# S5 + FoX decoder step: second memory weights among u's reads, output matrices between memory panels, last Toeplitz rows on two queues

## The reference, cut to what matters

```
mem_pairs = [mem_kv(mem_prompt, mem_norm[l], w_mem_kv[l]) for l in range(2)]   # rmsnorm(mem) @ w, 256 memory tokens
z = rmsnorm(x) @ w_in[0]; u = z[:, :768] as 48 groups of 16 channels
ar, ai, bbr, bbi = s5_discretize(...)            # 48 groups x 64 complex states
bu = einsum('btgc,gpc->btgp', u, bb)             # input to the state
h  = associative_scan over t of  h = a*h + bu    # complex
y  = einsum('btgp,gcp->btgc', hr, c_re) - einsum(..., hi, c_im) + d_skip*u
y  = gelu(y); y = y * sigmoid(y @ w_glu + b_glu)
```

## Time and profile before

| | us |
|---|---|
| Median of 3 runs (lowest, highest) | 1526.56 (1525.75, 1530.57) |
| The profiled execution | 1528.19 |
| Its span in the trace | 1526.4 |
| TensorE matmuls busy | 1418.7 (93%) |
| VectorE busy | 976.9 (64%) |
| ScalarE busy | 577.0 (38%) |
| GpSimd busy | 638.6 (42%) |
| Mean granted TensorE clock | 0.965 |

### The profile page before, as it was taken

The page is one execution under the profiler, slowest core; times in us unless marked ns, Lnnn a source line. Parts: engine busy times, 40 slices in busy tenths (PEclk is TensorE's granted clock), DMA queues, the critical chain, the costliest instruction groups (busy, mean ns, idle before and its releaser), DMA issues.

```text
span 1526.4 us, 32537 instructions
## 1 busy us (share of the span) xinstructions
PE 1418.7 (93%) x12097; PEld 1316.3 (86%) x12097; DVE 976.9 (64%) x1658; ACT 577.0 (38%) x1019; POOL 638.6 (42%) x420
## 2 busy tenths in 40 slices
PE   6986868989999999999899989998989999999997
PEld 6984758979999999999789966557889999999997
DVE  5759967576773177766658688662677761377755
ACT  4544354344342143423434235431444331234313
POOL 1686332304344334432269878302223443344430
PEclk9997789999999999999899999999999999999999
DMA  5344463213333232332236679994213233223321
GB/s 173 117 113 79 66 174 114 87 41 97 95 100 97 74 96 85 104 96 71 73 99 188 201 197 310 317 323 137 69 56 95 83 103 90 82 86 93 103 82 62
DMA packets 289082, 180.47 MB, mean 118 GB/s; under 512 B 54248, under 2 KB 274572, under 8 KB 288924
## 3 DMA queue, kind: packets, MB, share of 16 engines
q1 hardware_dynamic: 288412, 179.07, 40.8%
q10 hardware_dynamic: 576, 0.13, 0.0%
HBM read 167.10 MB, written 10.63 MB: 116 GB/s over the span
## 4 chain that ended last, share of the span: by engine, by line
PE 70%; DVE 14%; issue 9%; ACT 2%; DMA 2%; SPq 1%; POOL 1%; DVEq 0%; ACTq 0%; POOLq 0%
PE big L2641 57%; PE big L2707 3%; PE misc L2792 2%; PE big L2738 1%; DVE tmp L1253 1%; DVE y L1730 1%; DVE rstd L1211 1%; DVE x L1736 1%; DVE w_lo L1200 1%; DVE x_lo L1243 1%; PE misc L2762 1%; SPq L591 1%; ACT yc L2498 1%; PE big L2990 1%; PE misc L3207 1%
## 5 line engine op out<-in xcount | busy, mean ns | idle before, releaser
L941 POOL TENSOR_TENSOR w_lo<-raw,w_hi 128x1024 fp32r<-128x1024 f32 (+2 forms) x153 | 393.8, 2574 | 714.2 <-ACT w_hi L2136 553.8
L2136 ACT ACTIVATE w_hi<-raw 128x1024 fp32r<-128x1024 f32 (+2 forms) x179 | 198.5, 1109 | 586.7 <-PE big L2641 538.8
L2641 PE MATMUL big<-x_hi,w_hi 128*128 128x264 f32 x1984 | 406.7, 287 | 8.3 <-DVE uc L1819 2.8
L2641 PE MATMUL big<-x_hi,w_lo 128*128 128x264 f32 x1984 | 400.8, 283 | 0.0
L2641 PE MATMUL big<-x_lo,w_hi 128*128 128x264 f32 x1984 | 398.8, 283 | 0.0
L2641 PEld LDWEIGHTS big<-x_hi,w_hi 128*128 128x128 f32 x1984 | 305.9, 189 | 13.0 <-issue 4.8
L2641 PEld LDWEIGHTS big<-x_lo,w_hi 128*128 128x128 f32 x1984 | 305.6, 189 | 0.0
L2641 PEld LDWEIGHTS big<-x_hi,w_lo 128*128 128x128 f32 x1984 | 305.3, 189 | 0.0
L1823 DVE SCALAR_TENSOR_TENSOR yc<-uc,convw,yc 128x512 f32<-128x512 f32 x88 | 136.7, 1553 | 113.2 <-ACT yc L2498 113.2
L2641 PE MATMUL big<-h_hi,w_hi 128*128 128x264 f32 x616 | 125.0, 284 | 6.3 <-DVE h_lo L1838 6.3
L2641 PE MATMUL big<-h_lo,w_hi 128*128 128x264 f32 x616 | 123.9, 282 | 0.0
(11 more groups left out here) (432 smaller groups left out, 2335.3 us busy)
## 6 DMA issues: line engine op xcount, KB each, us to landing
raw<-in_w_up SPq DMA_DIRECT2D x88, 512.0 KB, 3.9
raw<-in_w_down SPq DMA_DIRECT2D x32, 704.0 KB, 4.7
areas<-in_cache_v SPq DMA_DIRECT2D x42, 384.0 KB, 4.9
areas<-in_cache_k SPq DMA_DIRECT2D x41, 384.0 KB, 4.4
raw<-in_w_in SPq DMA_DIRECT2D x16, 512.0 KB, 4.3
raw<-in_w_out SPq DMA_DIRECT2D x16, 512.0 KB, 4.2
raw<-in_w_kv SPq DMA_DIRECT2D x12, 512.0 KB, 4.3
spare<-in_cache_k SPq DMA_DIRECT2D x12, 384.0 KB, 4.4
```

The costliest lines, as they stand in the source:

```text
L941: pool.tensor_tensor(w_lo[slot][:, 0:kb, :], raw[slot][:, 0:kb, :], w_hi[slot][:, 0:kb, :].bitcast(F32), ALU.subtract).then_inc(lo_made, 1)
L2136: A.activation(w_hi[slot][:, 0:kb, :], raw[slot][:, 0:kb, :], ACT.Copy).then_inc(hi_made, 1)
L2641: ins = pe.matmul(big[2 * slot + b_][:, 0:c1 - c0], w[slot][:, k, :], r[:, c0:c1], start=(k == 0 and n_ == 0), stop=(k == kb - 1 and n_ == 2))
```

## The change

Three things move; none is added or taken away.

1. On SP, the load of memory panel 13 stands between the fifth and the sixth of u_load(0)'s ten reads instead of behind them.
2. On VectorE, the six operations of the first third's `cp` go into the loop over the memory panels: the first behind the read of panel 12, the second behind that of 13, two behind 14 and two behind 15 (`CP_AT`). In the first four turns the `mem_lo` of the fourth comes ahead of the read-and-round step of that turn's next panel. The two row_max of scores 0 and 1, which followed `cp`, now follow the first six products of the scan of third 0.
3. In the last third, SP issues the first four toep rows (16 to 64 KB) and ScalarE the last four (80 to 128 KB), right after its copies of `kern`.

```
+U_AHEAD = 5
+CP_AT = {4: (0,), 5: (1,), 6: (2, 3), 7: (4, 5)}
+ACT_TOEP = 4
-            def u_load(t):
+            def u_load(t, between=None):
                 g = slice(t * TG, t * TG + TG)
                 for tau in range(CHUNK):
+                    if tau == U_AHEAD and between is not None:
+                        between()
...
-            u_load(0)
-            weights("memkv1", mem_w[1], start=1)
+            u_load(0, lambda: weights("memkv1", mem_w[1], start=1, stop=2))
+            weights("memkv1", mem_w[1], start=2)
...
-                for tau in range(CHUNK):
+                for tau in range(CHUNK if t < THIRDS - 1 else CHUNK - ACT_TOEP):
                     load(toep[CH * tau:CH * tau + CH, :, (CHUNK - 1 - tau) * CH:P],
                          kern[:, :, 0:(tau + 1) * CH], "toep_in")
...
+            def cp_first(n):
+                a_r, a_i = (pw[:, 0:TP, 0:CHUNK + 1]... for pw in (pw_r, pw_i))
+                w_r, w_i = (cT[:, ri]... for ri in range(2))
+                tv = tmp[0][:]...
+                o_r, o_i = (cp[0][:, ri]... for ri in range(2))
+                if n == 0:
+                    dve.wait_ge(s_("cT_made"), 1)
+                    tt(o_r, a_r, w_r, ALU.mult)
+                elif n == 1:
+                    tt(tv, a_i, w_i, ALU.mult)
+                elif n == 2:
+                    tt(o_r, o_r, tv, ALU.subtract)
+                elif n == 3:
+                    tt(o_i, a_r, w_i, ALU.mult)
+                elif n == 4:
+                    tt(tv, a_i, w_r, ALU.mult)
+                else:
+                    do(V.scalar_tensor_tensor(o_i, o_i, -1.0, tv, ALU.mult, ALU.subtract))
+                    sync()
...
                 tell(V.scalar_tensor_tensor(dst, big[2 * (q % 2)][:, 0:NMEM], ..., rstd_mem[:],
                                             ALU.mult, ALU.mult), panel_read, q + 1)
+                if i == 3:
+                    mem_lo(1, (2 * m, 2 * m + 1))
+                for n in CP_AT.get(i, ()):
+                    cp_first(n)
                 if i + 2 < 8:
                     lo(q + 2)
-                if l == 0:
+                if i < 3:
                     mem_lo(1, (2 * m, 2 * m + 1))
-            dve.wait_ge(s_("cT_made"), 1)
-            s5_product(0, cp[0], (0, 1), CHUNK + 1, cT)
             mark(s_("cp_ready"))
-            row_max(0, 0)
-            row_max(0, 1)
...
                 cmul(w_[0], w_[1], e_r[:, js], e_i[:, js], v[:, 0, :, 0:NCH], v[:, 1, :, 0:NCH], w_[2], conj=True)
+                if t == 0:
+                    row_max(0, 0)
+                    row_max(0, 1)
...
+                if t == THIRDS - 1:
+                    act.wait_ge(s_("kern_ready"), 4 * THIRDS)
+                    act.wait_ge(s_("s5_zero"), 2)
+                    for tau in range(CHUNK - ACT_TOEP, CHUNK):
+                        act.dma_start(toep[CH * tau:CH * tau + CH, :, (CHUNK - 1 - tau) * CH:P],
+                                      kern[:, :, 0:(tau + 1) * CH]).then_inc(s_("toep_in"), 16)
```

More of the change, by code:

```diff
@@ L1574, in _ @@
                 beside_win0(m)
+            def cp_first(n):
+                a_r, a_i = (pw[:, 0:TP, 0:CHUNK + 1].unsqueeze(3).to_broadcast([P, TP, CHUNK + 1, CH])
+                            for pw in (pw_r, pw_i))
+                w_r, w_i = (cT[:, ri].unsqueeze(2).to_broadcast([P, TP, CHUNK + 1, CH]) for ri in range(2))
+                tv = tmp[0][:].rearrange("p (j n c) -> p j n c", n=CHUNK + 1, c=CH)
+                o_r, o_i = (cp[0][:, ri].rearrange("p j (n c) -> p j n c", c=CH) for ri in range(2))
+                if n == 0:
[12 more added lines that the diff above has]
+                    sync()
             tell(V.memset(u[0][:], 0.0), s_("u0_zero"), 1)
```

## The result

The changed kernel takes 1533.27 us (median of 19 runs, 1528.69 to 1539.06) against 1529.78 (19 runs, 1524.58 to 1535.05): a ratio of 1.0023 [1.0012, 1.0034], or +3.5 us [+1.8, +5.2]. The forecast was +1.5. Ratios and intervals here are estimates over all timed runs; they are not the quotient of the two medians, and differences in us given with an interval are worked out from them. The profiled execution of the changed kernel, 1528.69 us with a span of 1526.6, is the fastest of its 19 and comes within 0.5 us of that of before (1528.19, span 1526.4; 13 of the 19 runs of before were slower than that one). So the two traces do not show the loss in their ends, and the middle has to be read step by step.

The account below looks back on a forecast made before the run. In S5 VectorE was taken to bound, with GpSimd's table-to-b_used chain nearly as long; matmuls from 270 us. Weights 0, bp +3.0, rows -1.5 gave +1.5 us on 1526.56, so 1528.1; range 1519.0 to 1533.5.

Parts of the forecast that it names:

- No change beyond 0.3%: Whole kernel: time stays within 0.3% (4.6 us) of before; chance 0.56 including the case that the parts do nothing.
- GpSimd decides the start of bp: Second third's input matrices: VectorE must wait for GpSimd's b_used, whose chain had 0.8 us of air; memset ends at 126.2.
- +3.0 at bp: Second third's input matrices on VectorE start at 142.9 instead of 139.92, 3.0 us later; bounds -1.5 and +6.
- The table's delay: GpSimd's power table: +3.0 beside output-matrix products, +1.6 beside scan products; u[1]'s memset ends 4.6 us later.
- VectorE idle for 8 to 12 us: Sign of being right: VectorE idle that long before bp of the second third, released by GpSimd.
- Weights at nothing: Panel 13's weights among u's reads: last memory read 4.2 us earlier with the mem_lo move, GpSimd's chain no earlier; 0 us.
- Rows at -1.5: Last third's Toeplitz rows on two queues: last landing 1.9 us earlier, 1.5 us gained on the path; bounds 0 and -2.9.
- Sums within 3 us of hp: Sign of being right: output sums of the last third start less than 3 us after hp.
- The sum: Whole kernel: 0 for weights, +3.0 at bp, -1.5 for rows, together +1.5 us, giving 1528.1.
- the term that I left unpriced: TensorE's clock: a third's sums at the higher or lower level differ by 4.5 us either way; not in the forecast.
- The faster rival: b_used chain not binding or shrinking: -9 us, 1517.6; or second third's sums at the higher clock: -3; chance 0.20.
- The slower rival: GpSimd's table: u[1]'s memset over about 7 us later, or 5 with one clock drop; +6 us, 1532.6; chance 0.24.

Follow-up runs that it names:

- experiment 1: Changed kernel with GpSimd clearing u[1] before the last three steps of its power table: 1525.32 us against 1530.39, ratio 0.9971.
- 3: Kernel before, with GpSimd clearing u[1] five times instead of once: 1533.26 us, ratio 1.0026.
- 4: Kernel before with only the VectorE part (output matrices between panels, mem_lo ahead, later row_max): 1534.56 us, ratio 1.0031.
- 9: Kernel before with only panel 13's weights moved between u's fifth and sixth read: 1530.38 us against 1529.17, ratio 1.0001.
- experiment 5: Kernel before with only the last third's Toeplitz rows split over SP and ScalarE: 1529.6 us against 1530.14, ratio 0.9997.
- 7: As experiment 1, with ScalarE's copy_turned 6 ahead of its four Toeplitz issues: 1525.55 us, ratio 0.9975 against before.
- 6: As experiment 1, with all eight Toeplitz rows back on SP: 1527.51 us, ratio 0.9977 against before.
- 8: As 7, with SP's memory-key loads of the last third behind the Toeplitz rows: 1527.28 us, ratio 0.998 against before.

## Why the prediction was right, and where it was not

- **No change beyond 0.3%: right, by a small margin.** The interval reaches +5.2 us, past the 4.6 of 0.3%. And 1533.27 lies 0.2 us inside the upper end of the range, 1533.5: of the 5.2 us above the forecast of 1528.1, 3.2 are the baseline, which had 1526.56 in three runs and has 1529.78 in 19. That range did not hold what it was said to hold either; the bounds of the terms with one change of clock give 1517.7 to 1537.1.
- **GpSimd decides the start of bp: right.** Predicted memset end 126.2, measured 126.14; scan start near 117.0, measured 117.54; GpSimd's six products 2.9 us, measured 2.9 (139.23 to 142.14). c_turn(1) moved with c_in, to 139.21 from 135.29. Experiments 1 and 3 moved bp by moving that memset alone.
- **+3.0 at bp: slightly large.** Measured +2.33 (2.08 in 4). The 4.55 us at the reads of u shrank to 3.97 at c_in, because SP made up 0.6 us among its reads and stores. Less 0.8 for the quicker products and 0.8 of air gives 2.3. I had left SP's own stretch as it was.
- **The table's delay: right in sum, 4.55 for 4.6, by two errors that cancel.** The output-matrix products cost about 2.6 us and not 3.0, and not by three more stretched steps of 1 us: one 256-wide step more is stretched, and five 24-wide steps, which I had not counted, lose 1.7. I had also read only three stretched steps before; two more, at 105.59 and 110.42, lie beside VectorE's w_lo operations. A step beside the scan's products costs up to 0.33 more (0.94 against 0.61), where I took 0.2, and there are six of them and not eight: 1.9 for 1.6. The Trainium skill's "GPSIMD Engine Reference", Key points, names the shared interfaces as the cause; the traces agree, with 1.0 us for a step beside a 1.35 us product and 0.33 beside a 0.69 us one.
- **VectorE idle for 8 to 12 us: just short.** It was 6.98, and 7.9 with the 0.89 ahead of row_max. VectorE came later than the 132.4 that I predicted, at 135.27: its scan products stretched beside the table, and the last scores came from TensorE 0.89 us late, since each set took 2.07 us there, at the lower clock, where it took 1.13 before.
- **Weights at nothing: right.** 0.4 us at bp, a ratio of 1.0001. The last memory read was put at 110.4 and came at 110.82. The weights alone bring it forward by 0.8 us (9); the moved mem_lo and output matrices of 4 bring 3.1 (111.46).
- **Rows at -1.5: the mis-sized term.** Measured at the sums, -0.3 in the changed kernel's trace, nothing in 5 (ratio 0.9997), -1.0 at best (1 and 7 against 6). The step that failed is that the remaining head sums and queries "move 3 us into its own 6.16 us gap". ScalarE's issues took 3.9 to 4.9 us and not 3.0, and what TensorE does behind them ran at the lower clock (2.08 us for the queries), so that it filled the gap to the end and a little over. The other half was seen: the rows themselves landed only about 0.5 us earlier (last issue begun near 200.9, plus 6.3, against 203.2 plus 4.5). The Trainium skill's "DMA: Bandwidth & Descriptors", Issuing engines are not separate DMA queues, says that only the time of issuing is saved, and that the DMAs share the same engines. The trace agrees with both: 2.2 us were saved in issuing and 1.8 were lost in landing.
- **What I did not see in that term.** With TensorE's own work moved up against the sums, the first sums and queries of the last third run mostly at the higher level in the changed kernel, 1 and 5 (4.4 to 4.7 us instead of 7.5), and the chain that ended last passes over hp and GpSimd's add. From the last third's sums to mdst it is 31.9, 31.7 and 29.9 us there, 33.0 to 33.5 in the six traces with all rows on SP (7 and 8: 33.8 and 31.8). The timed runs do not show this gain beyond their noise.
- **Sums within 3 us of hp:** 3.15 us (204.41 to 207.56); just over.
- **The sum.** By the parts' ratios: +0.2 (weights), +4.7 [+2.6, +6.9] (output matrices), -0.5 (rows), together +4.4; whole change +3.5 [+1.8, +5.2]. The forecast of +1.5 lies just below that interval. With +2.3 at bp and -0.3 of rows the traces account for +2.0 of mechanism. The 1.5 us between that and the median are not accounted for. The clock was the term that I left unpriced, and the timed runs point at it: the mean granted clock over an execution has a median of 0.962 in the changed kernel's 19 (its profiled one had the highest, 0.967) and 0.961 in 4's 12, against 0.965 in the 35 runs of before beside 1 to 4. Among those 35 a clock lower by 0.001 goes with 0.7 us more, among the changed kernel's 19 with 1.2, so that 0.003 would be 2 us or more. That the edit lowers the clock, and where, no trace shows.
- **The faster rival** needed a b_used chain that did not bind; experiment 1 shows what it would have given, -4.4 us [-6.4, -2.3], half of the 9 that I wrote; 2.7 of the difference is VectorE's row, which ended at 135.1 and not at 132.4. The rest stays open.
- **The slower rival** asked for the memset 7 us later; it came 4.55 later. The median's interval still reaches past 0.3%, on this mechanism.

## What to carry to other kernels

When work is taken out of the row of the engine that bounds, follow back every semaphore that this engine waits for next, through every queue in program order: here a second chain (table, memset, reads, c_in) had 0.8 us of air, and the move of the products lengthened it. An edit that only loses may be half of one that gains: moving one memset ahead of the table's end turned +0.23% into -0.29%, while on the kernel before it gained nothing (1.0013 [1.0001, 1.0025]). A DMA issue put on a compute engine is paid in that engine's stream: ask who waits for its next instruction.

## What the runs showed of the hardware that was not expected

- VectorE pays too when both work at once. Its output-matrix products take 1.65 to 1.78 us beside the table and 1.36 beside GpSimd's memsets (before, 116.34 to 124.28). Its 0.69 us scan products took 0.99 to 1.09 beside GpSimd's steps (118.27 to 123.56 in the changed kernel), and 0.77 to 0.83 beside GpSimd's input products in experiment 1; with GpSimd at a memset or idle (127.29 to 131.61) they took 0.69.
- Issues on two queues at once take longer each. ScalarE's four took 0.89 us each (3.54, experiment 1), 0.97 (3.87, changed kernel) and 1.21 (4.85, experiment 5), SP's four beside them 0.87, 0.84 and 0.99, against 0.76 for SP's eight alone in the same third before (6.05) and 0.67 in the first third (5.35). ScalarE had the large rows and SP the small ones, so what part is the engine's and what the rows' isn't separated.
- Spreading eight rows out of 16 partitions over two queues did not raise their rate: 91 GB/s in the window 202 to 203 at a DMA share of 0.52, as much as the 91 of one queue. This is one microsecond of each trace; with the early memset single windows read 98 and 104 with two queues (1, 197 to 199) against 94 and 97 with one (6, 200 to 202).
- TensorE's sums of one third run at 0.48 us or at 0.76 in different executions: those of the second third turned to the higher level midway in the changed kernel's trace and stayed at the lower in experiment 4's, where the same work precedes them at nearly the same time. Behind the start of the last third's sums the level differs too: the first four pairs take 5.5 us before and 3.6 in the changed kernel.
